# Routed experts of a decoder trunk: rows gathered by quarters and turned on VectorE, next place's gate/up product ahead of a place's down product, place sizes alternating

## The reference

```python
def swiglu(x, w_gu, w_down):
    gate, up = jnp.split(x @ w_gu, 2, axis=-1)
    return (jax.nn.silu(gate) * up) @ w_down

    def block(acc, inp):
        tok, wt, ex = inp
        y = swiglu(x_pad[tok], w_gu[ex], w_down[ex])
        return acc.at[tok].add((y * wt[:, None]).astype(acc.dtype)), None
```

## Time and profile before

| | |
|---|---|
| median of three runs | 2622.13 us (2617.12 to 2624.11) |
| profiled execution, span | 2625.4 us |
| PE busy | 2519.5 us, 96% |
| PE weight load busy | 1555.6 us, 59% |
| DVE busy | 856.1 us, 33% |
| ACT busy | 460.9 us, 18% |
| POOL busy | 510.2 us, 19% |
| DMA | 382.73 MB, mean 146 GB/s |
| gate/up of the routed experts, L1799 | 4096 matmuls, 529.7 us busy |
| down of first (and two second) chunks, L1807 | 528 matmuls, 242.5 us |
| transposes of gathered rows, L1792 | 800, 91.8 us |

### The profile page before, as it was taken

One profiled execution on the slowest core, in us unless ns is written; L12 is line 12 of the kernel. 1 busy time (PEld: TensorE's weight loads), 2 busy tenths in 40 slices (PEclk: granted clock), 3 DMA queues, 4 the chain that ended last, 5 costly groups with the idle time before them and its releaser, 6 DMA issues. The chain is left out here.

```text
span 2625.4 us, 27939 instructions
## 1 busy us (share of the span) xinstructions
PE 2519.5 (96%) x11230; PEld 1555.6 (59%) x11230; DVE 856.1 (33%) x1539; ACT 460.9 (18%) x756; POOL 510.2 (19%) x454
## 2 busy tenths in 40 slices
PE   6999999999999999999999999999999999999992
PEld 3444554345899444444445544587777777788881
DVE  5001654655534433323323532211122222211115
ACT  1001223335453100100000110111112222111110
POOL 2000111101453000000001054022333333222221
PEclk9999999999999999999999999999999999999996
DMA  6101003100000310111130420499999999999984
GB/s 242 56 32 64 1 32 101 48 8 9 1 1 25 112 48 25 48 48 48 64 137 5 152 65 18 165 335 340 284 288 305 289 296 309 322 364 358 357 272 152
DMA packets 159182, 382.73 MB, mean 146 GB/s; under 512 B 14384, under 2 KB 34608, under 8 KB 158288
## 3 DMA queue, kind: packets, MB, share of 16 engines
q1 hardware_dynamic: 133200, 294.25, 31.5%
q0 software_dynamic: 24848, 79.68, 12.1%
q10 hardware_dynamic: 1008, 7.02, 0.7%
HBM read 320.14 MB, written 60.78 MB: 145 GB/s over the span
## 5 line engine op out<-in xcount | busy, mean ns | idle before, releaser
L1799 PEld LDWEIGHTS banks<-arena 128*128 128x128 f32 x4096 | 520.7, 191 | 45.3 <-issue 42.9
L1799 PE MATMUL banks<-arena 128*128 128x128 f32 (+7 forms) x4096 | 529.7, 290 | 2.7 <-DVE arena L2175 2.0
L1354 PE MATMUL banks<-arena 128*128 128x512 f32 x672 | 293.2, 597 | 1.3 <-PEq L710 1.3
L307 PE MATMUL banks<-arena 128*128 128x512 f32 x640 | 280.9, 596 | 4.7 <-DVE arena L1067 4.3
L2219 POOL DMA_INDIRECT acc_scratch<-arena x99 | 153.0, 1545 | 607.2 <-DMA acc_scratch<-arena 349.1
L1807 PE MATMUL banks<-arena 128*128 128x512 f32 (+1 forms) x528 | 242.5, 602 | 1.6 <-DVE arena L2178 0.9
L1354 PEld LDWEIGHTS banks<-arena 128*128 128x128 f32 x672 | 128.4, 191 | 163.9 <-issue 163.7
L307 PEld LDWEIGHTS banks<-arena 128*128 128x128 f32 x640 | 120.2, 190 | 159.2 <-issue 149.5
L300 PE MATMUL banks<-arena 128*128 128x512 f32 x384 | 168.7, 597 | 0.6 <-PE banks L300 0.6
L1383 PE MATMUL banks<-arena 128*128 128x512 f32 x384 | 166.7, 592 | 0.0
L2156 DVE TENSOR_TENSOR arena<-arena,banks 128x256 f32<-128x256 f32 (+7 forms) x63 | 29.1, 462 | 421.9 <-PE banks L1799 416.9
(11 more groups left out here) (356 smaller groups left out, 2580.7 us busy)
## 6 DMA issues: line engine op xcount, KB each, us to landing
arena<-in_exp_w_gu SPq DMA_DIRECT2D x64, 2048.0 KB
arena<-in_exp_w_down SPq DMA_DIRECT2D x64, 1024.0 KB, 12.4
arena<-in_w_in SPq DMA_DIRECT2D x10, 2048.0 KB, 9.1
arena<-in_w_in SPq DMA_DIRECT2D x12, 1024.0 KB
arena<-in_w_branch SPq DMA_DIRECT2D x12, 512.0 KB
arena<-in_x SPq DMA_DIRECT2D x4, 1024.0 KB, 14.9
h_scratch<-arena SPq DMA_DIRECT2D x1, 4096.0 KB, 11.1
arena<-in_w_out SPq DMA_DIRECT2D x2, 2048.0 KB, 7.9
```

Source lines behind the costliest of these rows:

```text
L307: last = nc.tensor.matmul(PS[:, bank, :], wt[:, k, ct * P:(ct + 1) * P], hT[:, k, half * HALF:(half + 1) * HALF], start=(k == 0), stop=(k ...
L1354: last = nc.tensor.matmul(PS[:, g % 4, :], lhs[:, k, :], rhs[:, k, :], start=(k == 0), stop=(k == 3))
L1799: last = nc.tensor.matmul(PS[:, bank + part, f * n:(f + 1) * n], weights[:, k, part * FF + f * P:part * FF + (f + 1) * P], by_k(x, n)[:, k ...
```

## The change

Five things change, all in the last stage but for the pads.

1. Rows are gathered by quarters. `hx_scratch` holds rows of 1024 floats, seen by the gather as four rows of 256; the gates get a table of their own (`gt_scratch`). For 32 tokens one gather brings the four quarters of each to 4 x 32 partitions. A first chunk takes four gathers and one for the gates, a second chunk one for each begun 32 rows (always over 128 partitions) and one for the gates. A second table of indices, `quad_i`, is made beside `slot_i`, with one GpSimd copy, four small products and one VectorE instruction.
2. DVE turns them: one `transpose` of 32 x 32 blocks for each chunk (`turn`) from the gathered rows to `xT`, without PSUM. PE's transposes and the two copies go, but for the spill loop. The contraction rows stand in another order, so the gate/up weights are loaded in that order too: four loads of 32 partitions in place of one of 128.
3. On PE gate/up of place r + 1 now comes ahead of down of place r (`hidden`). The places take three pairs of banks in turn (`pair`), 0 to 5.
4. The places are taken in another order (`place_order`): sizes with and without a second chunk spread evenly, so 128, 216, 128, 216, 128, 192 rows and so on.
5. On POOL the adds of a place come four places behind the gathers, and the second chunk's add doesn't wait for the first's. The padding rows are 256 and not 128.

```diff
+def place_order():
+    double = [r for r in range(NE - 1) if rank_rows(r) > P]
+    single = [r for r in range(NE - 1) if rank_rows(r) == P]
+    at = {r: (i + 0.5) / len(double) for i, r in enumerate(double)}
+    at.update({r: i / (len(single) - 1) for i, r in enumerate(single)})
+    return sorted(range(NE - 1), key=lambda r: (at[r], r)) + [NE - 1]
...
+                def gate_up_in(dst, e, done):
+                    for q in range(4):
+                        sp.dma_start(dst[32 * q:32 * (q + 1), :, :],
+                                     gu_v[bass.ds(e, 1), q].rearrange("a j c n -> j (a c) n")).then_inc(done, 16)
...
-                    sp.dma_start(gu[r % RING], gu_v[bass.ds(e, 1)].rearrange("a p k n -> p (a k) n")).then_inc(x_wg[r % RING], 16)
+                    gate_up_in(gu[r % RING], e, x_wg[r % RING])
...
+                def hidden(r):
+                    n = place_rows(r)
+                    pe.wait_ge(x_wg[r % RING], 64 * (r // RING) + 64)
+                    pe.wait_ge(x_xt, chunks(r + 1))
+                    if r >= 3:
+                        pe.wait_ge(x_hid, r - 2)
+                        pe.wait_ge(x_ya, chunks(r - 2))
+                        pe.wait_ge(x_yv, chunks(r - 2))
+                    x = by_k(xT[r % 2], width(r))
+                    gate_up(gu[r % RING], x, n, pair(r), 0).then_inc(x_g, 1)
+                    gate_up(gu[r % RING], x, n, pair(r), 1).then_inc(x_u, 1)
...
-                rows_in(0)
-                more_rows_in(0)
+                pe.wait_ge(f_int, 1)
+                hidden(0)
                 for r in range(NS):
...
-                    if r + 1 < NS:
-                        rows_in(r + 1)
+                    if r == 1:
+                        pe.wait_ge(f_pr, 2 * NT)
+                    if r + 1 < NS:
+                        hidden(r + 1)
                     pe.wait_ge(x_hid, r + 1)
...
+                def turn(rows, r, lo, n):
+                    x = by_k(xT[r % 2], width(r))[:, :, lo:lo + 32 * n].rearrange("p c (g i) -> p g c i", i=32)
+                    src = rows[r % 2][:, 0:n * QD].rearrange("p (g c j) -> p g c j", g=n, j=32)
+                    nc.vector.transpose(x, src).then_inc(x_xt, 1)
+
+                def rows_in(r):
+                    if r >= 2:
+                        v.wait_ge(x_u, r - 1)
+                    v.wait_ge(x_inA[r % 2], landed(r, False))
+                    turn(xgA, r, 0, 4)
+                    if more(r):
+                        v.wait_ge(x_inB[r % 2], landed(r, True))
+                        turn(xgB, r, P, groups(r))
...
+                    if r + 1 < NS:
+                        rows_in(r + 1)
                     v.wait_ge(x_sl, r + 1)
                     v.wait_ge(x_u, r + 1)
+                    if r >= 2:
+                        v.wait_ge(x_dn, chunks(r - 1))
...
+                def gather_place(r):
+                    block, i = 2 * PLACES[r], r % 2
+                    for g in range(4):
+                        gather(xgA[i][:, g * QD:(g + 1) * QD], hq_d, quad_i[:, g * P + block:g * P + block + 1], P, x_inA[i])
+                    gather(gtA[i], gt_d, slot_i[:, block:block + 1], P, x_inA[i])
+                    if more(r):
+                        for g in range(groups(r)):
+                            gather(xgB[i][:, g * QD:(g + 1) * QD], hq_d, quad_i[:, g * P + block + 1:g * P + block + 2], P, x_inB[i])
+                        gather(gtB[i], gt_d, slot_i[0:more(r), block + 1:block + 2], more(r), x_inB[i])
...
+                gather_place(0)
+                gather_place(1)
+                for r in range(2, NS + 3):
+                    if r < NS:
+                        pool.wait_ge(x_xt, chunks(r - 1))
+                        pool.wait_ge(x_gate, chunks(r - 1))
+                        gather_place(r)
...
+                    if 0 <= r - 4 < NS:
+                        add_place(r - 4)
+                add_place(NS - 1)
```

More of the change, by code:

```diff
@@ L25 @@
 FF = 256
-HX = D + NE
 OVB = NE
@@ L322, in _ @@
                 sp.dma_start(ring[1], w_cols(R_GROUPS[1], W)).then_inc(r_w[1], 16)
-                sp.dma_start(pad_id, row("pad_id", 0, P)).then_inc(a_pad, 16)
+                for i in range(2):
+                    sp.dma_start(pad_id[:, i * P:(i + 1) * P], row("pad_id", 0, P)).then_inc(a_pad, 16)
                 sp.wait_ge(a_zero, 1)
[L325 to L330, removed]
+                for i in range(2):
+                    pads = slice(SEQ + i * P, SEQ + (i + 1) * P)
+                    sp.dma_start(hx_d[pads, :], zero).then_inc(pads_in, 16)
+                    sp.dma_start(acc_d[pads, :], zero).then_inc(pads_in, 16)
+                    sp.dma_start(gt_d[pads, :], zero[:, 0:NE]).then_inc(pads_in, 16)
+                sp.wait_ge(a_zero, 2)
+                sp.dma_start(slot_d.rearrange("(b p) a -> b (p a)", p=2 * P), pad_id[0:NBLK // 2, :]).then_inc(pads_in, 16)
                 sp.wait_ge(a_h, NT)
@@ L1560, in more, with groups, width, landed @@
         def more(r):
-            return rank_rows(r) - P
+            return place_rows(r) - P
+        def groups(r):
+            return -(-more(r) // 32)
+        def width(r):
+            return P + 32 * groups(r)
+        def landed(r, second):
+            return sum(16 * ((groups(q) if second else 4) + 1) for q in range(r % 2, r + 1, 2) if more(q) or not second)
         def chunks(r):
             return sum(2 if more(q) else 1 for q in range(r))
+        def pair(r):
+            return 2 * (r % 3)
         def table(eng, ap, i, most):
@@ L1786, in _ @@
                         pe.wait_ge(f_sl2, 32)
+                        pe.wait_ge(f_slq, 1)
                         nc.tensor.transpose(PS[:, 0, 0:P], slot_f, ident)
-                        nc.tensor.transpose(PS[:, 0, P:NBLK], spill_f[0:OVB, :], ident[0:OVB, 0:OVB]).then_inc(f_stp, 1)
-                def transposes(rows, n):
-                    for k in range(KD):
-                        last = nc.tensor.transpose(PS[:, k // 4, (k % 4) * n:(k % 4 + 1) * n], rows[0:n, k * P:(k + 1) * P],
-                                                   ident[0:n, 0:n])
-                    return last
+                        nc.tensor.transpose(PS[:, 0, P:NBLK], spill_f[0:OVB, :], ident[0:OVB, 0:OVB])
+                        for g in range(4):
+                            last = nc.tensor.matmul(PS[:, 1, g * P:(g + 1) * P],
+                                                    slot_q[:, g * P:(g + 1) * P], ident, start=True, stop=True)
+                        last.then_inc(f_stp, 1)
                 def gate_up(weights, x, n, bank, part):
@@ L1866, in _ @@
                     down(dn[r % RING], by_f(hidT[r % 2], n), 0, P, 6).then_inc(x_dn, 1)
-                    if r + 1 < NS and more(r + 1):
-                        more_rows_in(r + 1)
-                    own = 2 + 2 * (r % 2)
                     if more(r) > 64:
-                        down(dn[r % RING], by_f(hidT[r % 2], n), P, more(r), own).then_inc(x_dn, 1)
+                        down(dn[r % RING], by_f(hidT[r % 2], n), P, more(r), pair(r)).then_inc(x_dn, 1)
                     elif more(r) > 32:
-                        down_two(dn[r % RING], by_f(hidT[r % 2], n), more(r), own).then_inc(x_dn, 1)
+                        down_two(dn[r % RING], by_f(hidT[r % 2], n), more(r), pair(r)).then_inc(x_dn, 1)
                     elif more(r):
-                        down_four(dn[r % RING], by_f(hidT[r % 2], n), more(r), own).then_inc(x_dn, 1)
+                        down_four(dn[r % RING], by_f(hidT[r % 2], n), more(r), pair(r)).then_inc(x_dn, 1)
                 n = n_spills(pe)
                 with pe.Fori(0, n) as j:
-                    pe.wait_ge(s_in, 16 * j + 16)
-                    pe.wait_ge(x_xa, chunks(NS))
-                    pe.wait_ge(x_xv, chunks(NS))
-                    transposes(xg_spill, P).then_inc(s_xt, 1)
+                    pe.wait_ge(s_in, 32 * j + 32)
+                    pe.wait_ge(x_hid, NS - 2)
+                    pe.wait_ge(x_ya, chunks(NS - 2))
+                    pe.wait_ge(x_yv, chunks(NS - 2))
+                    for k in range(KD):
+                        last = nc.tensor.transpose(PS[:, k // 4, (k % 4) * P:(k % 4 + 1) * P], xg_spill[:, k * P:(k + 1) * P], ident)
+                    last.then_inc(s_xt, 1)
                     pe.wait_ge(s_w, 32 * j + 32)
```

210 lines of the change are left out of this document (96 added, 114 removed).

## The result

| | before | after |
|---|---|---|
| median | 2620.5 us, runs beside after | 2932.5 us (2918.3 to 2963.4) |
| ratio to before | 1 | 1.116 (95% interval 1.113 to 1.120) |
| span of the profiled execution | 2625.4 us | 2916.5 us |
| granted TensorE clock, mean | 0.986 | 0.938 |
| PE busy | 2519.5 us | 2545.0 us |

The change made the kernel 12% slower. One of the four runs of after, the one of 2963.4 us, was in a slower state and is left out of the ratio; the other three have a median of 2930.8. The time lies far above the forecast of 2550 us and above the range. Read the page's slices of after first: PE, its granted clock, the DMA share and the rate.

What follows compares the result with a forecast made beforehand. PE and a full DMA side were taken as two limits in the experts' stage. 2625.4 - 80 (PE) + 8 (limits meeting) = 2553, less 3 from profiled execution to median: 2550 us, range 2525 to 2760.

Steps and rivals of the forecast that it cites:

- the price of the four loads: Gate/up weight loads of 32 partitions: each 2 KB packet taken at today's 86 ns, range up to 172 ns.
- The rival: Four gate/up loads of 32 partitions are slow, two engines sharing one way in: 2715 us, slower; chance 0.36.
- engines drift apart: Reason for pricing the slow loads at half, +165 us, where all engines meeting would cost 333 us, 2880.
- PE's own sum: Experts' stage on PE: 93 us of gains less 13 us at the start, 80 us less.
- the gains: Experts' stage: PE's transposes (79 us), gather waits (11) and the wait before the first gate/up (3) go, 93 us.
- Start: Second place's gate/up load: PE stands still about 13 us (11 to 16), until 1698 us.
- Meeting of two equal limits: End of the experts' stage: PE and the DMA side finish nearly together, adding 8 us (0 to 25).
- Gathers by quarters: Row gathers for a 128-row chunk: 1.73 us plus 0.25 for the gates, against 1.46 for whole rows.
- the rival of dear gathers: Gathers' 1 KB packets at twice 54 ns add 107 us, 2650 us; chance 0.06.
- GpSimd's chain and VectorE's turn: Issue of gathers and adds, and the turning of rows, stay hidden: cost 0, bound 25 us for GpSimd.
- The rival of GpSimd's chain: GpSimd sets the pace: double places cost some 2 us more, 72 us in all, 2622 us, no change; chance 0.10.
- that case: The likeliest case alone, whole kernel: 2550 us, reaching from 2530 to 2590; chance 0.48, all of it faster.

Runs made afterwards that it cites:

- e1: The changed kernel with gate/up weights in one load of 128 partitions again, normalised rows stored permuted instead; 2565.3 us, 0.977 of before.
- e3: As e1, but gate/up weights in four loads of 32 neighbouring partitions, natural row order; 2969.4 us, 1.132 of before.
- e5: As e3, but two loads of 64 partitions, 0 to 63 and 64 to 127; 2949.2 us, 1.125 of before.
- e14: As e1, but half of each expert's gate/up weights left out from place 5 on (output wrong); 2549.9 us, 0.973 of before.
- e2: As e1, but gate/up weights in four 512 KB loads, each over all 128 partitions; 2563.0 us, 0.977 of before.
- e6: As e3, but each of the four loads takes every fourth partition; 2754.4 us, 1.051 of before.
- e4: The kernel before with only its gate/up load changed, to four loads of 32 partitions; 2901.8 us, 1.106 of before.
- e9: The kernel of e1 unchanged, measured again on another occasion; 2694.1 us, 1.027 of before.

## Why the prediction was wrong

**The step that failed** is the price of the four loads. The prediction bounded a 2 KB packet between 86 and 172 ns and took 86, "the row of the same packets". The same packets to other partitions are not the nearest row: they measured 136 ns over all of q1. If the down loads still cost 42 us a megabyte, which no run shows apart, gate/up's two of every three cost (3 x 66 - 42) / 2 = 78 us, 160 ns a packet, near the upper end. That is what the step had wrong: in after PE waited 279 us for these loads, and with the loads over 128 partitions again (e1) 28 us. The rival named the mechanism, and what was to show it came out: waits for gate/up weights all along, under 340 GB/s, q1's packets well over 86 ns.

**The rival's own price was wrong too.** It was halved from 2880 to 2715 because "engines drift apart". The runs show nothing of it: e3, e5 and after are at 2932 to 2969, above even the full price. That full price, 333 us, is near the measured difference by luck: it has 62 us too much for q1 and nothing for the neighbours, the transfers of the other queue. Against e1, q1's 198 MB at 66 for 43 us cost 198 x 23 / 16 / 1.05 = 271 us. And q0, whose gathers and adds are the same in both, costs 75 us a megabyte for 61: 82 x 14 / 16 / 1.05 = 68 us. Together 339, against 352.7 between the two spans. Seen from PE the same sum is 279.1 - 28.0 = 251 us more waiting for weights, and 634.2 - 535.0 = 99 us from the lower clock: 350 us. The prediction had no term for PE's clock, which its idle time pulls down; here it probably adds nothing, since the DMA side sets the pace and a faster PE would only wait longer; that is argued, not tried.

**The rest of the sum,** read from e1 and e14:

- PE's own sum: -80 us forecast. e14's span is 2547.7 against 2625.4, -78. Right, with the start's 17.5 us in it, so that the gains were 95 for 93.
- Start: 13 us forecast, bounds 11 to 16; the wait is 17.5. PE was to have its weights at 1698 and had them at 1703.75: the 6.3 MB did not move at 360 GB/s, the rate of a long full stretch. Mechanism right, size low.
- Meeting of two equal limits: 8 us (0 to 25) forecast, 15 measured (e1 against e14).
- Gathers by quarters: priced at 1.73 + 0.25 us for 1.46. In e1 q0 costs 61 us a megabyte, before 59 in a full stretch. So they cost little extra, and the rival of dear gathers is out; the 54 ns of the earlier trace rows, from 1 KB packets of another load, were too much for these. (q0 holds the adds too, so this is a price of the mixture.)
- GpSimd's chain and VectorE's turn: cost 0 forecast. In e1 POOL's gathers and adds are busy 542 us (405 x 0.97 + 99 x 1.55 = 546 was the forecast without the gaps), a turn of 128 x 1024 takes 1.25 us as taken, and PE waited 0.3 us for a turn (so too in after, L2134 in the row above). The rival of GpSimd's chain is out: in e1, with the same 405 gathers, PE had no gap from 1830 to 2290.
- The sum without the failed step was 2550, the kernel with that step undone takes 2564 to 2566 us on three occasions, inside the 2530 to 2590 given for that case, and 2694 on one, far outside: the prediction had no term for the standstills.

**The chances.** 0.40 for slower with the reason named was not far off, but the range ended at 2760 because the rival was halved. Before halving a price, one should have a row that shows the halving.

## What to carry to other kernels

Write a large load over all 128 partitions. If it must be cut, cut it otherwise than by blocks of partitions (e2), or take sets spread through them (e6, shown by its price alone); blocks of 32 or 64 neighbours cost 1.6 times as much of the DMA engines here and made the other queue's gathers late. If a layout forces such blocks, permute the small tensor (here the normalised rows, once) and leave the large one (here every expert's weights) as it is. When a bound has two ends a factor of two apart, and the DMA side is full, take neither from a row that differs in the one thing that changes: measure that transfer, or forecast the dearer case with its full price.

## What the runs showed of the hardware

- Four 512 KB loads of 128 partitions equal one of 2 MB (2563 and 2565 us); of 32 neighbouring partitions they cost 1.56 times as much engine time a megabyte (67 against 43 us), of every fourth 46, where one load costs 45 at the same DMA share.
- A slow queue can make its neighbour slow: the same gathers by quarters and adds went from 61 (e1) to 75 us a megabyte (e3). With gathers of whole rows it was 66 and 68 (before, e4), yet PE's waits for them went from 11 to 145 us.
- Gathering rows of 1 KB, four for each token, was hardly dearer a byte than rows of 4352 bytes: 61 against 59 us a megabyte of q0 on a full side, adds included.
- TensorE can stand still for up to 1.9 us inside a product with nothing in the trace to wait for (e6, e9), and starts again at evenly spaced instants. The kernel before took 2620 to 2622 us (median) on every occasion. The one-load kernel took 2565 us on three and 2694 on one; a kernel whose TensorE has no gaps should be measured on more than one.
